# A transformer layer on one core: the first period of an output product, and the border behind it, in another order

## The reference, cut to what matters

```python
q = (cq @ w_uq).reshape(B, S, MLA_HEADS, MLA_NOPE + MLA_ROPE)
kv = (ckv @ w_ukv).reshape(B, S, MLA_HEADS, MLA_NOPE + MLA_V)
...
o = causal_softmax_attention(q, k, v, (MLA_NOPE + MLA_ROPE) ** -0.5)
y = o.reshape(B, S, MLA_HEADS * MLA_V) @ w_o
h = layer_norm(ALPHA * h + y, ln_g[i, 0], ln_b[i, 0])
h = layer_norm(ALPHA * h + jnp.square(jax.nn.relu(h @ mlp_w1[i])) @ mlp_w2[i], ln_g[i, 1], ln_b[i, 1])
```

## Time and profile before

| | us |
|---|---|
| median of 3 runs (1837.59 to 1838.71) | 1837.93 |
| the profiled execution, its own time | 1839.09 |
| span of the profiled execution | 1837.3 |
| TensorE busy | 1800.4 |
| VectorE busy | 1509.8 |
| ScalarE busy | 924.5 |
| GpSimd busy | 179.9 |
| TensorE's wait for a load of `o_act`, the longest of its waits | 3.6 |

### The profile page before, as it was taken

One profiled execution on the slowest core, in us unless ns is written; L12 is line 12 of the kernel. 1 busy time (PEld: TensorE's weight loads), 2 busy tenths in 40 slices (PEclk: granted clock), 3 DMA queues, 4 the chain that ended last, 5 costly groups with the idle time before them and its releaser, 6 DMA issues.

```text
span 1837.3 us, 28144 instructions
## 1 busy us (share of the span) xinstructions
PE 1800.4 (98%) x10916; PEld 1617.9 (88%) x10916; DVE 1509.8 (82%) x1850; ACT 924.5 (50%) x1168; POOL 179.9 (10%) x100
## 2 busy tenths in 40 slices
PE   9999999989999999999999999999999999999994
PEld 8888898968889999999999999988888888888883
DVE  3156777697999888888888888889889999999997
ACT  5256667543356655565565556543433343333434
POOL 3343322100020000000000000000011111100003
PEclk9999999999999999999999999999999999999998
DMA  6223343598324656456545654678465474654712
GB/s 232 81 81 101 122 136 104 190 328 289 139 81 161 212 206 220 175 180 215 205 171 197 218 185 173 239 301 335 151 265 209 188 285 156 260 206 185 295 70 91
DMA packets 130995, 350.68 MB, mean 191 GB/s; under 512 B 7536, under 2 KB 79600, under 8 KB 112496
## 3 DMA queue, kind: packets, MB, share of 16 engines
q1 hardware_dynamic: 57104, 275.14, 40.1%
q10 hardware_dynamic: 73824, 74.74, 12.3%
HBM read 268.06 MB, written 81.79 MB: 190 GB/s over the span
## 4 chain that ended last, share of the span: by engine, by line
PE 91%; DVE 5%; DMA 1%; issue 1%; ACT 1%; POOL 0%; POOLq 0%; DVEq 0%; ACTq 0%
PE bank L2030 30%; PE bank L2034 29%; PE bank L2035 29%; PE bank L2201 1%; DVE w_lo L1412 1%; DVE w_lo L1771 1%; DMA o_kept<-o_lo 1%; PE bank L2193 0%; PE bank L2191 0%; PE bank L2062 0%; DMA o_act<-o_kept 0%; DVE acc L1831 0%; POOL acc L690 0%; ACT acc L1200 0%; DVE small L1522 0%
## 5 line engine op out<-in xcount | busy, mean ns | idle before, releaser
L2030 PE MATMUL bank<-up_hi,w_hi 128*128 128x256 f32 x1808 | 512.5, 283 | 0.4 <-issue 0.4
L2034 PE MATMUL bank<-up_lo,w_hi 128*128 128x256 f32 x1808 | 512.0, 283 | 0.0
L2035 PE MATMUL bank<-up_hi,w_lo 128*128 128x256 f32 x1808 | 512.0, 283 | 0.0
L1170 ACT ACTIVATE w_hi<-d_b 128x1024 fp32r<-128x1024 f32 x192 | 202.1, 1061 | 316.3 <-PE bank L2035 255.9
L2030 PE MATMUL bank<-w_hi,down_act 128*128 128x512 f32 x896 | 349.2, 390 | 1.8 <-DVE acc L1831 1.2
L2034 PE MATMUL bank<-w_lo,down_act 128*128 128x512 f32 x896 | 348.6, 389 | 0.0
L2035 PE MATMUL bank<-w_hi,down_act 128*128 128x512 f32 x896 | 348.6, 389 | 0.0
L2030 PEld LDWEIGHTS bank<-up_hi,w_hi 128*128 128x128 f32 x1808 | 347.6, 192 | 0.9 <-issue 0.7
L2034 PEld LDWEIGHTS bank<-up_lo,w_hi 128*128 128x128 f32 x1808 | 347.6, 192 | 0.0
L2035 PEld LDWEIGHTS bank<-up_hi,w_lo 128*128 128x128 f32 x1808 | 347.5, 192 | 0.0
L964 ACT ACTIVATE w_hi<-up_b 128x1024 fp32r<-128x1024 f32 x180 | 186.9, 1054 | 157.0 <-PE bank L2035 129.0
(11 more groups left out here) (184 smaller groups left out, 2822.3 us busy)
## 6 DMA issues: line engine op xcount, KB each, us to landing
up_b<-up_weights SPq DMA_DIRECT2D x128, 512.0 KB, 4.8
d_b<-down_weights SPq DMA_DIRECT2D x64, 1024.0 KB, 5.3
down_act<-acts_kept SPq DMA_DIRECT2D x56, 1024.0 KB, 4.8
acts_kept<-h_hi ACTq DMA_DIRECT2D x32, 896.0 KB, 6.0
acts_kept<-h_lo ACTq DMA_DIRECT2D x32, 896.0 KB, 6.7
raw<-weights SPq DMA_DIRECT2D x46, 512.0 KB, 3.3
o_b<-out_weights SPq DMA_DIRECT2D x16, 1024.0 KB, 6.8
o_act<-o_kept SPq DMA_DIRECT2D x14, 1024.0 KB, 7.7
```

What stands on the lines that cost most here:

```text
L1170: act.activation(w_hi[:, DOWN_SLOT[n], :], source[:, ab, :], ACT.Copy).then_inc(down_hi, 1)
L2030: first_pass = pe.matmul(out_, a_hi, b_hi, start=start, stop=False, skip_group_check=more)
L2034: pe.matmul(out_, a_hi, b_lo, start=False, stop=False, skip_group_check=more)
L2035: return pe.matmul(out_, a_lo, b_hi, start=False, stop=stop, skip_group_check=more)
```

## The change

In the output product's first period VectorE makes T1 ahead of the heads' sums and splits step 3's low parts around them; `head_parts_lo` comes after step 4's low parts; the low parts of period 1's step 0 come ahead of the evictions of step 5 and of T3 and T1 for period 1. ScalarE makes the high parts of units 6 and 7 ahead of `head_parts_hi` and those of units 10 and 11 ahead of the low store. SyncE issues B22 and B12 for period 1 later and B11 after the last load of `o_act`. At the border the second half of A12's low part goes from VectorE to GpSimd; row 3 is normalised in two parts on ScalarE; the last four transposes (n = 12 to 15) move behind step 4, and affines and splits are interleaved accordingly.

```diff
@@ sync @@
             sp.wait_ge(w_split, N_HB)
+
+            sp.wait_ge(o_w_lo, 5)
             load_o(o_b22[1], 1, 2, o_b22_loaded[1])
-            sp.wait_ge(o_w_lo, 4)
             sp.wait_ge(o_w_lo_b, 4)
             load_o(o_b12, 1, 1, o_b12_loaded)
+            sp.wait_ge(o_stored, 32 * PAIRS)
+            load_o_act(0, 6)
             sp.wait_ge(o_t_made, 8)
             load_o(o_b11, 1, 0, o_b11_loaded)
-            sp.wait_ge(o_stored, 32 * PAIRS)
-            load_o_act(0, 6)
@@ gpsimd @@
+            part = slice(4, 8)
+            pool.wait_ge(up_act_hi, 4)
+            pool.tensor_tensor(up_act[A12][1][:, part, :], norm_t[:, HK + 4:HK + 8, 0, :],
+                               up_act[A12][0][:, part, :].bitcast(f32), ALU.subtract).then_inc(up_act_lo_12[1], 1)
@@ scalar @@
             attention(PAIRS - 1, False)
-            for n in (4, 5):
+            for n in range(4, 8):
                 o_weights(0, n)
             head_parts_hi(PAIRS - 1)
             store_heads(PAIRS - 1, 0)
-            for n in range(6, 10):
+            for n in range(8, 12):
                 o_weights(0, n)
             store_heads(PAIRS - 1, 1)
...
             root_of(3, slice(2, 4))
-            normalise_row(3)
+            normalise_row(3, (0, 1))
             for g in range(2):
                 affine(HK + 2 * g)
...
-            for n in (HK + 4, HK + 6):
-                affine(n)
+            normalise_row(3, (2, 3))
             for g in range(2):
+                affine(HK + 4 + 2 * g)
@@ vector @@
+            def first_o_period():
+                o_evicts(0, 0)
+                o_rest(0, 2)
+                o_t1_made(0)
+                o_rest_part(0, 3, 0)
+                head_sums(PAIRS - 1)
+                o_rest_part(0, 3, 1)
+                o_evicts(0, 1)
+                o_evicts(0, 2)
+                o_rest(0, 4)
+                head_parts_lo(PAIRS - 1)
+                o_evicts(0, 3)
+                o_rest(0, 5)
+                o_t4_made(0)
+                o_evicts(0, 4)
+                o_rest(0, 6)
+                o_rest(1, 0)
+                o_evicts(0, 5)
+                o_t3_made(1)
+                o_t1_made(1)
...
+            left_lo_part(up_act[A12], norm_t[:, :, 0, :], HK, 2, 0, up_act_lo_12[0])
             o_evict_p7(1)
-            for g in range(2):
-                left_lo_part(up_act[A12], norm_t[:, :, 0, :], HK, 2, g, up_act_lo_12)
...
-            for half in range(2):
-                normalise_part(2, HB * half, HB)
-            for n in (HK + 1, HK + 3):
-                affine(n)
-            dve.wait_ge(t_act, HK // 2 + 2)
+            normalise_part(2, 0, HB)
+            affine(HK + 1)
+            normalise_part(2, HB, HB)
+            affine(HK + 3)
             left_lo(a21, norm_t[:, :, 1, :], 0, 4)
-            for n in (HK + 5, HK + 7):
-                affine(n)
-            left_lo(up_act[A22], norm_t[:, :, 1, :], HK, 6)
+            affine(HK + 5)
+            left_lo_part(up_act[A22], norm_t[:, :, 1, :], HK, 6, 0, up_act_lo)
+            affine(HK + 7)
+            left_lo_part(up_act[A22], norm_t[:, :, 1, :], HK, 6, 1, up_act_lo)
@@ tensor @@
                 pe.wait_ge(o_evicted, LAST_O + 16)
-                for n in range(HK, 2 * HK):
+                for n in range(HK, HK + 4):
                     transpose_rows(n)
                 pe.wait_ge(t_act, HK // 2)
                 pe.wait_ge(t_dve, HK // 2)
                 plain_step(0, 4, (up_act_lo, 2))
+                for n in range(HK + 4, 2 * HK):
+                    transpose_rows(n)
```

More of the change, by code:

```diff
@@ L320, in mla_mlp_program @@
         sum_made = sem("sum_made")
-        up_act_hi, up_act_lo, up_act_lo_12 = sem("up_act_hi"), sem("up_act_lo"), sem("up_act_lo_12")
+        up_act_hi, up_act_lo = sem("up_act_hi"), sem("up_act_lo")
+        up_act_lo_12 = sem("up_act_lo_12"), sem("up_act_lo_12_pool")
         b12_loaded = sem("b12_loaded")
@@ L510, in _ @@
             sp.wait_ge(sum_made, 6)
-            sp.wait_ge(up_act_lo_12, 2)
+            sp.wait_ge(up_act_lo_12[0], 1)
+            sp.wait_ge(up_act_lo_12[1], 1)
             load_up(b11[1], 3, 0, b11_loaded[1])
@@ L926, in _ @@
             for q in range(O_PERIODS):
-                for n in range(10 if q == 0 else 0, UNITS if q < O_PERIODS - 1 else UNITS - 2):
+                for n in range(12 if q == 0 else 0, UNITS if q < O_PERIODS - 1 else UNITS - 2):
                     o_weights(q, n)
@@ L1102, in plain_pairs, with normalise_row @@
                 store_hidden(1, 1)
-            def normalise_row(t):
+            def normalise_row(t, which=None):
                 act.wait_ge(row_scaled, 1 + t // 2)
                 pieces = 2 if t == 1 else CG
-                for i in range(pieces):
+                for i in which or range(pieces):
                     part = rows[:, t, D // pieces * i:D // pieces * (i + 1)]
@@ L1526, in measure_parts @@
                     measure_part(first + t, col)
+            def first_o_period():
[18 more added lines that the diff above has]
+                o_t1_made(1)
             def o_period(q):
                 last = q == O_PERIODS - 1
-                if q:
-                    o_evicts(q - 1, 6)
-                    o_rest(q, 1)
-                    o_t2_made(q)
+                o_evicts(q - 1, 6)
+                o_rest(q, 1)
+                o_t2_made(q)
                 o_evicts(q, 0)
@@ L1546, in o_period @@
                 o_rest(q, 3)
-                if q == 0:
-                    head_parts_lo(PAIRS - 1)
-                if 0 < q and not last:
+                if not last:
                     o_t4_made(q)
@@ L1552, in o_period @@
                 o_rest(q, 4)
-                if q == 0 or last:
+                if last:
                     o_t4_made(q)
@@ L1694, in _ @@
             o_t2_made(0)
-            for q in range(O_PERIODS):
+            first_o_period()
+            for q in range(1, O_PERIODS):
                 o_period(q)
@@ L2363, in plain_step @@
                 for k in range(HK):
-                    if ready and k % 4 == 0:
+                    if ready == up_act_lo_12 and k % 4 == 0:
+                        pe.wait_ge(ready[k // 4], 1)
+                    elif ready and k % 4 == 0:
                         pe.wait_ge(ready[0], ready[1] + k // 4 + 1)
```

5 lines of the change are left out of this document (1 added, 4 removed).

## The result

The changed kernel takes 1849.37 us (median of 5 runs, 1846.20 to 1853.05) beside 1837.93 (1834.99 to 1839.20) of the kernel before, measured in turn on one chip: a ratio of 1.0064 with a 95% interval from 1.0050 to 1.0078, or 11 to 12 us slower. One run of all that follow, of the experiment tp_ahead, took 8474 us and is left out of its ratio. The forecast was 1842.8 with a range up to 1848.0: the sign is right, the size is not. The profiled execution of the change took 1849.37 us, its span 1847.6, which is 10.3 more than the span behind the earlier trace rows.

The account below looks back on a forecast made before the run. TensorE bounds the kernel, working 1800.4 of 1837.3 us, so only its waits and low clock count. Terms 0 + 3.6 + 0 + 1.3 = +4.9 on the median 1837.93 gave 1842.8 us, range 1836.5 to 1848.

Parts of the forecast that it names:

- the store's landing in period 0: Output product, period 0: low store issued at 401.9, step 6 starts at 414.4 as before; 0 us, ends -2.0 and +4.9.
- so no more is paid: Behind the border: second plain pair's first weights' low part due at 574.3, before TensorE's 575.1; no further cost.
- The border's term: Border to the MLP: step 4 starts sooner, step 6 waits 1.3 us for its second half; +1.3, ends -0.4 and +1.9.
- TensorE's wait before unit 6: Output product, period 0: TensorE goes on from unit 5 at once, 1.7 us gained, then lost in a longer idle.
- I take 5.8: Period 0: estimated time of the heads' low store from issue to landing, 5.8 us, ends 4.1 and 9.7.
- a start of 0.6: Period 0: start cost of 0.6 us within the low store's estimate, beside 5.2 us for bytes at 383 GB/s.
- at its least 4.1: Period 0: least time of the low store, 4.1 us, where it took 9.68 before the change.
- congestion: Rival, period 0: store takes 9.7 and load 7.7 again; +4.9 more, 1847.7 us; chance 0.12.
- Light queues: Rival, period 0: store takes 4.1, load 6.4, step 6 begins 2.0 sooner, clock holds; +0.9, 1838.8 us; chance 0.24.
- Period 1's start, +3.6: Output product, period 1: TensorE waits for VectorE, 2.5 us at unit 2, 0.3 at unit 4, plus 0.8 for clock.
- 0 to 2.5; I take 0.8: Period 1: cost of a lower clock after the 2.5 us stop, put at 0.8 us.
- A12's half on GpSimd, term 0: Border: GpSimd's half ends at 549.5, before TensorE wants it at 549.8; 0 us, ends 0 and 0.4.

Follow-up runs that it names:

- tp_ahead: Kernel before with the change's border edits, but transposes 12 to 15 back ahead of step 4: 1840.01 us, ratio 1.0013.
- after: First profiled execution of the changed kernel, with no further edit: 1849.37 us, span 1847.6.
- loads_behind: Changed kernel with the loads of period 1's B22 and B12 behind the load of step 6's left factor: 1847.92 us, ratio 1.0061.
- t3_first: Changed kernel with period 1's T3 ahead of the low parts of that period's step 0: 1847.83 us, ratio 1.0057.
- the record: The recorded execution of the kernel before, which the forecast was made from: 1839.09 us, span 1837.3.
- keep_first: Changed kernel with ScalarE's copy of the third pair's kept product ahead of the second plain pair's hidden_hi: 1848.29 us, ratio 1.0057.
- best: Changed kernel with earlier heads' low store, later B22 and B12 loads, earlier T3 and B21 in period 1, and only the GpSimd half at the border: 1838.19 us.
- oprod_only: Kernel before with the output product's part of the change alone: 1844.79 us, ratio 1.0039.
- before_again: Kernel before, unchanged, profiled once more: 1840.66 us.
- a12_only: Kernel before with only the border's GpSimd half of A12's low parts, VectorE's half ahead of its last eviction: 1835.82 us, ratio 0.9990.
- whole_row: Kernel before with the change's border edits, but the rows normalised as before, transposes 12 to 15 still behind step 4: 1842.64 us, ratio 1.0025.
- after_again: Changed kernel, unchanged, profiled once more: 6.16 us over the record from unit 0 to unit 20.

## Why the prediction was wrong

The forecast was +4.9 us and the measured change +11.4. Three things in it failed: the store's landing in period 0 (term 0; 1.2 to 2.0 came), the sentence "so no more is paid" behind the border (1.8 came), and the single execution that all terms were set against (some 2). The border's term was 1.0 too small.

**TensorE's wait before unit 6: right.** 1.7 us was forecast, 1.63 to 1.68 came in every kernel with T1 ahead.

**Period 0, term 0: the step that failed was the store's landing.** Unit 0 started 1.74 us later in after than in before, so times are compared relative to unit 0. By that clock the loads of B22 and B12 left when the forecast had them (399.26 less 1.74 is 397.5; forecast 397.6), and the store left at 400.8, 1.1 sooner than the forecast's 401.9, because it didn't wait for the end of unit 11's high part. "I take 5.8" was the error: it took 8.27, and 8.9 to 9.4 in the other four executions. The load then took 6.5 for 6.7. Together -1.1 + 2.5 - 0.2 = 1.2 us, which is what after shows at unit 12.

Most of the 2.5 can be worked out from the forecast's own rows. A store that leaves 1.1 sooner has 1.1 us more of the loads' bytes still ahead of it. And "a start of 0.6" contradicts "at its least 4.1": 0.9 MB at 383 GB/s are 2.4 us, so a store with nothing beside it (4.08 in loads_behind) spends 1.7 us on something else. 5.8 + 1.1 + 1.1 = 8.0, an estimate, where 8.27 came. The rate was lower than 383 GB/s too: 347 GB/s from 401 to 409 us in after. Whether the three DMAs went one behind the other or shared the rate decides little here, since the store landed last (the loads at 405.50 and 408.61, the store at 410.79); what splits the other executions' 8.9 to 9.4 from 8.3 stays open. That the loads cause the long store is shown by the kernels in which they leave behind it (4.1, 4.2, 5.1). The rival "congestion" was nearest for the store (9.7) and took too long a load (7.7; it took 6.5). The term is 1.2 to 2.0 in place of 0.

The Trainium skill says that a lighter load on the memory makes a DMA's fixed cost of about 2 us smaller (DMA: Bandwidth & Descriptors, "Latency and other measured facts"). These traces agree in direction, 4.1 us for the lightest store and 9.4 for the most crowded. The spread of 5.3 us is more than the whole fixed cost that the page speaks of, so that cost alone can't be what decides it. "Light queues", the rival that this rule favoured, did not come, because the queues were not light. Its own support holds in the trace of before, though the earlier trace rows mix stores and loads: the low stores of the first five pairs took 4.1 us each.

**Period 1's start, +3.6: right in mechanism and size, with the clock undersized.** The wait at unit 2 was 1.9 to 2.3 (forecast 2.5), and t3_first removes it by moving T3 alone; up to unit 20 after lost 0.45 more (forecast 0.3). Of the clock, the forecast had "0 to 2.5; I take 0.8": it fell in three of four executions and cost 1.7 each time. From unit 12 to 20 the four executions have 2.6, 4.2, 4.2 and 4.2 over the record.

**A12's half on GpSimd, term 0: right.** The transposes of the lower rows come 0.5 us sooner (forecast 0.4), and GpSimd's half ran from 547.1 to 549.6 on before's time (553.09 to 555.59 less 6.0), in time for 549.8.

**The border, +1.3: the mechanism right, the size 2.3.** Step 4 began 2 us sooner (565.18 less the 6.0 by which all was late there is 559.2; forecast 559.1), the new wait in step 6 was 1.63 for 1.3. Of the 1.0, 0.5 is in the lower rows' chain (7.8 us from step 4's end to the end of the second low part, for "7.3 with small gaps"), 0.1 in step 4 and 0.1 in its start; 0.2 more is the forecast's own weighing, which had 1.5 with the low clock, took 1.3, and got the low clock.

**"So no more is paid": wrong, 1.8 us.** In the prediction's words the low part of the second plain pair's first weights is due at 574.3, before TensorE's 575.1, and that was so: TensorE does not wait there. But the forecast followed VectorE's lateness to the second plain pair's weights and stopped there. It went on through squares, sums and a store to a wait for that store on ScalarE, 44 us later, behind which a copy for TensorE stood. tp_ahead breaks that chain at its beginning and keep_first at its end, and in both the wait goes.

**The record as base.** Some 2 us of the miss (1.6 and 0.45) are in no single term: all was set against one execution whose low-clock stretches behind unit 0 were long, while the change's own are as long or longer in nearly every execution. The forecast's "as before" at both places carried the record's chance over to the new kernel as nothing lost. Adding to the median did not mend it, because the median of before has that chance averaged out (1836.6 over the 84 runs here) and the terms have not.

Here is the sum in the forecast's order, as means over executions: 1.7 (store, net of the gain at unit 6) + 3.8 (period 1) + 1.6 (record, output product) + 2.1 (border) + 0.45 (record, border) + 1.7 (third pair) = 11.4. The first of these terms was forecast as 0, the second as 3.6, the fourth as 1.3, the others not at all.

**Still open.** It is open why four executions have 0.34 to 0.69 us in "rest" and the others nothing (in after TensorE waits 0.98 for an eviction at 527 us, where most wait 0.57). It is open too whether B11's landing could be hidden in best with fewer bytes in flight; that was not tried.

## What to carry to other kernels

Price a transfer on the queues by what leaves within a few microseconds on either side of it, and look for who releases those: here an edit that delays a store by 3.8 us also lets two loads of 1 MB leave together 3 us ahead of it. When pricing it, take the time of the same transfer alone from the trace, not its bytes at the peak rate. Follow a lateness on an engine that is not the bottleneck until its queue has run empty, past the first consumer that is in time: what it meets 40 us later may be a wait that stands ahead of something the bottleneck needs. And where the clock falls in waits, take the base from several executions before a term of 2 us is called nothing.

## What was not expected of the hardware

A stretch ahead of the output product runs partly at the lower clock in every execution but the record, in code that all kernels share. The profile counts TensorE as busy throughout. Windows of 20 us, first the record, then oprod_only:

```profile
60.00:80.00 20.00, 20.00 (x106) 17.14 (x105) 0.16 (x1) 5.55 (x8) 6.51 (x4) 1.00 0.24 80
```

```profile
60.00:80.00 20.00, 20.00 (x92) 17.03 (x91) 0.16 (x1) 3.09 (x4) 6.17 (x3) 0.83 0.17 56
```

The granted clock over these 20 us is 1.00 in the record and 0.91 or 0.83 in the other 17 executions. "Busy" hides what stands just before the fall: 32 matmuls of one column each, which take 3.5 to 4.7 us up to the next large one. Here they are in before_again, whose next rows start 0.43 us apart, the lower level, for seven rows (7 to 14 in the 17 executions). The record has the same 32 in 3.49 us and goes on at 0.23, so they precede the fall but don't settle it; no run here tried them otherwise.

```profile
66.17 3.69 PE L2062 MATMUL bank<-ones,square 128*128 128x1 f32 x32
...
70.29 0.63 PE L2034 MATMUL bank<-act_lo,w_hi 128*128 128x512 f32 x1
70.72 0.63 PE L2035 MATMUL bank<-act_hi,w_lo 128*128 128x512 f32 x1
```

With other such stretches unit 0 comes up to 3.8 us later than in the record, whatever the kernel (in keep_first 0.05 sooner). So here the record was at the short end, while behind unit 0 it was at the long one. That is one source of the spread of before's runs (1830.5 to 1842.3 us).

A wait of some 2 to 3.6 us doesn't settle whether the clock falls: in period 0 it fell after 3.63 us (record) and stayed at 1.00 after 3.0 (a12_only) and 3.2 (whole_row); in period 1 it stayed after 2.34 (after) and fell after 2.08 (after_again).
